# Channel-major products as 256-column matmuls onto one accumulator, and another first load

## The reference

```python
def reference(x, ...):
    hn = rmsnorm(h, norm_mix_w)
    z, xbc, dt_raw, u, g_a, g_b = split(hn @ w_in)        # 3072, 5120, 48, 1024, 2048, 2048 columns
    y_a = mamba2_mixer(z, xbc, dt_raw, ...)               # causal conv, silu, SSD over 8 groups, gated by silu(z)
    y_b = s5_mixer(u, ...)                                # complex scan per channel, gelu, GLU
    merged = sigmoid(g_a) * y_a + sigmoid(g_b) * y_b
    h = h + merged @ w_out
    h = h + conv_glu_ffn(rmsnorm(h), w_up, w_down)        # 5632 wide
    return rmsnorm(h)
```

## Time and profile before

| | |
|---|---|
| median of 3 runs | 1673.08 us |
| profiled execution | 1673.03 us |
| its span, first to last instruction | 1671.3 us |
| TensorE matmul busy | 1661.6 us, 99% of the span |
| VectorE busy | 1315.7 us, 79% |
| ScalarE busy | 984.2 us, 59% |
| granted TensorE clock, mean | 0.999 |

### The profile page before, as it was taken

How to read it: one execution, slowest core, us unless ns; L and a number is a source line. 1 busy time by engine, 2 the same in 40 slices (tenths; PEclk the granted TensorE clock), 3 DMA queues, 4 the chain that set the end, 5 groups by cost and what they waited for, 6 DMA issues and landing times.

```text
span 1671.3 us, 24189 instructions
## 1 busy us (share of the span) xinstructions
PE 1661.6 (99%) x8216; PEld 1386.3 (83%) x8216; DVE 1315.7 (79%) x1723; ACT 984.2 (59%) x1365; POOL 234.9 (14%) x337
## 2 busy tenths in 40 slices
PE   9999999999999999999999999999999999999998
PEld 8888888888888888888888888888888888888886
DVE  7999999999999996545766868888878888845544
ACT  7676676666677877444547754444444454454554
POOL 7843342221111110000000200000000000000001
PEclk9999999999999999999999999999999999999999
DMA  7666766666857666666787577777777777766564
GB/s 255 214 196 197 207 202 202 191 196 180 248 201 252 218 223 205 197 192 208 243 254 223 176 233 241 237 245 243 243 244 242 243 233 243 232 190 198 191 189 127
DMA packets 182873, 361.61 MB, mean 216 GB/s; under 512 B 17520, under 2 KB 45456, under 8 KB 182672
## 3 DMA queue, kind: packets, MB, share of 16 engines
q1 hardware_dynamic: 169264, 340.23, 64.0%
q0 software_dynamic: 12336, 19.92, 5.1%
q10 hardware_dynamic: 1200, 0.53, 0.1%
HBM read 335.41 MB, written 18.92 MB: 212 GB/s over the span
## 4 chain that ended last, share of the span: by engine, by line
PE 74%; DVE 2%; ACT 1%; issue 0%; DVEq 0%
PE psum L1930 23%; PE psum L1931 23%; PE psum L1932 23%; PE psum L1915 2%; PE psum L1917 1%; PE psum L2051 1%; DVE wlo L1216 1%; PE psum L2052 0%; DVE dec L1566 0%; ACT whi L740 0%; PE psum L2058 0%; PE psum L1966 0%; DVE dec L1562 0%; ACT xtok L949 0%; DVE zx L1629 0%
## 5 line engine op out<-in xcount | busy, mean ns | idle before, releaser
L740 ACT ACTIVATE whi<-raw 128x1024 fp32r<-128x1024 f32 x580 | 612.6, 1058 | 583.2 <-PE psum L1932 472.0
L1216 DVE TENSOR_TENSOR wlo<-raw,whi 128x1024 fp32r<-128x1024 f32 x580 | 708.8, 1228 | 312.6 <-ACT whi L740 305.9
L1915 PE MATMUL psum<-act,whi 128*128 128x512 f32 x1088 | 342.5, 396 | 0.0
L1930 PE MATMUL psum<-whi,nw 128*128 128x512 f32 x704 | 274.1, 389 | 0.0
L1931 PE MATMUL psum<-wlo,nw 128*128 128x512 f32 x704 | 273.9, 389 | 0.0
L1932 PE MATMUL psum<-whi,nw 128*128 128x512 f32 x704 | 273.9, 389 | 0.0
L1917 PEld LDWEIGHTS psum<-act,wlo 128*128 128x128 f32 x1088 | 204.4, 188 | 48.3
L1917 PE MATMUL psum<-act,wlo 128*128 128x256 f32 x1088 | 213.7, 278 | 0.0
L1915 PEld LDWEIGHTS psum<-act,whi 128*128 128x128 f32 x1088 | 165.6, 189 | 3.3 <-issue 3.2
L1932 PEld LDWEIGHTS psum<-whi,nw 128*128 128x128 f32 x704 | 132.1, 188 | 27.6
L1930 PEld LDWEIGHTS psum<-whi,nw 128*128 128x128 f32 x704 | 132.1, 188 | 27.3
(11 more groups left out here) (255 smaller groups left out, 2236.7 us busy)
## 6 DMA issues: line engine op xcount, KB each, us to landing
raw<-in_w_up SPq DMA_DIRECT2D x176, 512.0 KB, 4.8
raw<-in_w_zx SPq DMA_DIRECT2D x96, 512.0 KB, 3.7
raw<-in_w_down SPq DMA_DIRECT2D x88, 512.0 KB, 4.3
raw<-in_w_gate SPq DMA_DIRECT2D x64, 512.0 KB, 5.2
raw<-in_w_proj SPq DMA_DIRECT2D x48, 512.0 KB, 4.4
raw<-in_w_bc SPq DMA_DIRECT2D x32, 512.0 KB, 3.9
raw<-in_w_glu SPq DMA_DIRECT2D x32, 512.0 KB, 4.5
raw<-in_w_out SPq DMA_DIRECT2D x32, 512.0 KB, 4.7
```

What stands on the lines that cost most here:

```text
L740: fn(whi[:, s, :], raw[:, s, :], ACTF.Copy).then_inc(hi_ready, 1)
L1216: V.tensor_tensor(wlo[:, s, :], raw[:, s, :], whi[:, s, :], ALU.subtract).then_inc(lo_ready, 1)
L1915: mm(psum[:, b + t, :], whi[:, s, cols(t)], x, start=first, stop=False)
L1930: mm(banks[:, t, :], x_hi, high[:, k], start=first and k == 0, stop=False)
```

## The change

- `unit`: the 512-column product on `whi` becomes two of 256 columns (activation high, activation low) that go, like the product on `wlo`, to columns 0 to 255 of the bank. A quad is now six matmuls of 256 columns. The sum of a group stands finished in PSUM.
- ScalarE's `take_sums` replaces `take_hsum`: it copies the sum straight to `ub`, `bc` or `cpad`, or applies silu on the way to `zx` for z groups, and its `sum_ready` frees the banks. `add_halves`, `group_sums`, `u_sums`, `cpad_free` go from VectorE, the separate silu of z from ScalarE; `residual` adds the PSUM sum to `h` in one step, with no copy by ScalarE.
- SyncE first loads the first half of weight unit 0, then x's first piece, the second half, then unit 1, x's second piece and so on. ScalarE and VectorE make each half of `whi` and `wlo` ahead of the two activation rows. 13 small products stand at the start instead of 17.

```diff
@@ SyncE
+            sp.dma_start(raw[:, 0, 0:2 * L], a["w_u"][0][:, 0:2 * L]).then_inc(w_first, 16)
             for c in range(4):
                 sp.dma_start(xin[:, 4 * c:4 * c + 4, :], a["x"][:, 4 * c:4 * c + 4, :]).then_inc(x_in[c], 16)
-                sp.dma_start(raw[:, c, :], a["w_u"][c]).then_inc(w_in[c], 16)
+                if c == 0:
+                    sp.dma_start(raw[:, 0, 2 * L:], a["w_u"][0][:, 2 * L:]).then_inc(w_in[0], 16)
+                if c < 3:
+                    sp.dma_start(raw[:, c + 1, :], a["w_u"][c + 1]).then_inc(w_in[c + 1], 16)
@@ ScalarE
-            def take_hsum(g, end, gi=0, ui=0):
+            def take_sums(to, g, end, gi=0, ui=0, func=ACTF.Copy):
                 act.wait_ge(unit_used, ui + end)
-                if g:
-                    act.wait_ge(sum_ready, gi + g)
-                fn(hsum[:, :, :], sums(g, 1), ACTF.Copy).then_inc(hsum_ready, 1)
+                fn(to, sums(g), func).then_inc(sum_ready, 1)
...
+            def group_sums(name, i, r):
+                _, per, quads, u0, g0 = phase(name)
+                func = ACTF.Copy
+                if name == "u":
+                    to = ub[:, 2 * (r + 1):2 * (r + 1) + 2, :]
+                elif name == "zx" and r % 2 == 0:
+                    to, func = zx[:, ds(i * 4 + r, 2), 0, :], ACTF.Silu
+                elif comes_late(name, i, r):
+                    to = bc[:, i * 4 + r, :, :]
+                else:
+                    to = cpad[:, :, 3:3 + L]
+                take_sums(to, g0 + r, u0 + (r + 1) * quads, i * per, i * (per * quads), func)
@@ VectorE
-            def add_halves(to, g, gi=0):
-                dve.wait_ge(hsum_ready, gi + (g + 1))
-                V.tensor_tensor(to, sums(g, 0), hsum[:, :, :], ALU.add).then_inc(sum_ready, 1)
...
-                dve.wait_ge(hsum_ready, g + 1)
-                mul(hg, hg, hsum[:, :, :], ALU.add)
-                V.tensor_tensor(hg, sums(g, 0), hg, ALU.add).then_inc(sum_ready, 1)
+                dve.wait_ge(unit_used, UNIT0[name] + 4 * r + 4)
+                V.tensor_tensor(hg, sums(g), hg, ALU.add).then_inc(sum_ready, 1)
@@ TensorE
                     for t in tiles:
-                        mm(psum[:, b + t, :], whi[:, s, cols(t)], x, start=first, stop=False)
+                        mm(psum[:, b + t, 0:L], whi[:, s, cols(t)], x_hi, start=first, stop=False)
+                        mm(psum[:, b + t, 0:L], whi[:, s, cols(t)], x_lo, start=False, stop=False)
                     for t in tiles:
-                        ins = mm(psum[:, b + t, L:2 * L], wlo[:, s, cols(t)], x[:, 0:L], start=False, stop=last)
+                        ins = mm(psum[:, b + t, 0:L], wlo[:, s, cols(t)], x_hi, start=False, stop=last)
...
-            for k in range(17):
+            for k in range(13):
                 mm(WARM, ones[:, :], ones[:, :], start=True, stop=True)
```

More of the change, by code:

```diff
@@ L303, in group_bank, with sums @@
             return 2 * (g % 2)
-        def sums(g, half):
+        def sums(g):
             b = group_bank(g)
-            return psum[:, b:b + 2, half * L:half * L + L]
+            return psum[:, b:b + 2, 0:L]
         def chunk_banks(name, c):
@@ L768, in _ @@
             fn(rs[:, 0:1], ones[:, 0:1], ACTF.Copy)
[L769 removed]
             for c in range(4):
[L771 removed]
                 for half, done in ((0, half_hi), (1, hi_ready)):
+                    act.wait_ge(w_first if c == 0 and half == 0 else w_in[c], 16)
+                    w = slice(half * 2 * L, half * 2 * L + 2 * L)
+                    fn(whi[:, c, w], raw[:, c, w], ACTF.Copy).then_inc(done, 1)
+                    if c == 0 and half == 0:
+                        act.wait_ge(parm_in, 16)
+                    act.wait_ge(x_in[c], 16)
                     for k in range(4 * c + 2 * half, 4 * c + 2 * half + 2):
                         weighed_hi(k)
[L775 to L777 removed]
             for c in range(4):
@@ L781, in _ @@
                 split_hi(n)
-            take_hsum(0, 4)
-            def group_hsum(name, i, r):
+            take_sums(ub[:, 0:2, :], 0, 4)
+            def group_sums(name, i, r):
                 _, per, quads, u0, g0 = phase(name)
-                take_hsum(g0 + r, u0 + (r + 1) * quads, i * per, i * (per * quads))
+                func = ACTF.Copy
[8 more added lines that the diff above has]
+                take_sums(to, g0 + r, u0 + (r + 1) * quads, i * per, i * (per * quads), func)
             def normed_hi(c):
@@ L858, in group_silu @@
                 _, per, quads, u0, g0 = phase(name)
-                if name == "u":
+                if name == "u" or name == "zx" and r % 2 == 0:
                     return
[L861 to L865, removed]
+                if name == "zx":
                     act.wait_ge(conv_done, i * 2 + (r // 2 + 1))
@@ L896, in mixer_turn @@
                     last = name == "bc" and i == 1 and r == per - 1
-                    group_hsum(*before)
+                    group_sums(*before)
                     hi(0)
@@ L1248, in _ @@
                     V.tensor_tensor(wlo[:, c, w], raw[:, c, w], whi[:, c, w], ALU.subtract).then_inc(done, 1)
+                    if c == 0 and half == 0:
+                        dve.wait_ge(parm_in, 16)
+                    for k in range(4 * c + 2 * half, 4 * c + 2 * half + 2):
+                        weighed_lo(k)
             dve.wait_ge(wdt_in, 64)
@@ L1422, in s5_out @@
                 V.scalar_tensor_tensor(to, to, col("s5_d", blk), sums_at, ALU.mult, ALU.add).then_inc(y5_out, 1)
[L1424 to L1433, removed]
             def group_conv(name, i, r):
@@ L1467, in late_add @@
                     ins.then_inc(conv_done, 1)
[L1469 to L1474, removed]
             def x_turned(g):
@@ L1516, in mixer_turn @@
                         lo(2)
-                    cpad_free(*before)
                     s5_turn_on(r)
@@ L1520, in mixer_turn @@
                         last_state_sum(blk)
-                    if r == per - 1 and not last:
-                        group_sums(name, i, r)
                     if not last:
```

31 lines of the change are left out of this document (10 added, 21 removed).

## The result

The changed kernel takes **1686.38 us** (median of 6 runs, 1686.09 to 1686.87) against 1673.09 us before (6 runs on the same chip): ratio 1.008, 95% interval 1.0067 to 1.0093. It is 13.3 us slower, where the forecast was 7.3 us faster.

What follows compares the result with a forecast made beforehand. The prediction took TensorE's matmul pace to bound the kernel. Gains of 6.1 (quads), 0.8 (start) and 0.4 us (wait before L2010) summed to 7.3, taking 1673.1 to 1665.8 us, range 1660 to 1680.

Steps and rivals of the forecast that it cites:

- The bound: Whole kernel: between start and end it goes at the pace of TensorE's matmuls; VectorE follows closely without holding it.
- Term 1: 608 quads: six 256-column products at 0.1145 us each make a quad 0.687 instead of 0.697 us; gain 6.1 us.
- Rival 2: 608 quads: fixed cost per matmul makes a quad 0.733 us, 21.9 us lost, 1693.8 us; chance 0.15.
- its point of decision, 0.1165: Quads: the 256-column pitch in us from which a fixed cost per matmul decides against the change.
- the lower bound of half the wide pitch: Quads: 256 columns take half the 512-column pitch, 0.1132 us; quad 0.679 us, gain 10.9 us.
- The floor from the weight loads: Quads: weight loads limit the 256-column pitch, put at 0.108 to 0.118 us from sixteen 128-column products and their loads.
- Term 2: Start: half a weight unit ahead of x lets TensorE start at about 6.7 us, not 7.76; gain 0.8 us.
- Rival 4: Start: x's second piece comes late, TensorE waits between u0's units; 0.8 us less gain, 1666.6 us; chance within forecast's 0.60.
- The small products: Start, before u0: 13 instead of 17 end between 6.54 us and 1.3 us sooner, covered by the wait for x.
- Term 3: Group sums: ScalarE no busier, VectorE loses 38 steps, some 26 us, worth nothing itself; 0.4 us gained before L2010.
- Rival 1: Quads: loads or small per-matmul costs take the gain; pitch 0.1155 to 0.118 us, 1669.4 to 1678.6 us; chance 0.19.
- Rival 3: Gate phase after the mixer: VectorE and ScalarE lag, term 1's gain becomes waits before L2051; 1669 to 1672 us; chance 0.06.

Runs made afterwards that it cites:

- the split alone: Kernel before with only the 512-column product on `whi` split into two of 256, written to the two bank halves as before: 1686.19 us, ratio 1.0077.

## Why the prediction was wrong

**The bound: right.** The pace of the matmuls was named as what counts, and it is all that counted: 14.2 us from the quads against 13.3 measured, and 0.4 us of the difference is the wait at L2010.

**Term 1: wrong, and of the other sign.** The step that failed is "I take 0.1145 us, between the first two, nearer to the pair". The pair of 256-column products in the earlier trace rows is 0.23 us from its first start to the next wide product, but starts beside a change of length don't give the price, and only the quad's 0.697 was sure; in a long stream the pitch is 0.1200. That is 0.0055 us more on each of 3648 products than the prediction took, 20 us, and all but a little of the distance from 1665.8 to 1686.4. Rival 2 had the right reading, a cost beyond the columns for each matmul with its load, and its point of decision, 0.1165, was passed. Its size was too large: it charged the whole rest of the quad to the narrow products (0.1221, 21.9 us), while 0.6967 - 2 × (0.2267 + 0.1200) = 0.0034 us of the quad come with the mixture of lengths and don't follow into a uniform stream. So a quad gets two more constants, 0.0267 us, and is rid of 0.0034: 0.0233 us more. Columns / 2.4 GHz plus what the earlier trace rows leave, 0.2264 - 512 / 2400 = 0.0131, would have given 0.1198 us and 608 × (0.719 - 0.697) = 13.4 us. That sum was to be had from the rows; the lower bound of half the wide pitch assumed that nothing is fixed, which no row supported, and the range of 1660 to 1680 left rival 2 out.

The floor from the weight loads, 0.108 to 0.118 us, was too low: sixteen products of 128 columns are not a stream of 256-column ones. Both stand above the 107 ns for a load that the prediction took from the Trainium skill ("TensorE: Matmul & The Clock Gate", LDWEIGHTS), and on both sides only of half the wide pitch, 0.1132 us. The Trainium skill's N / 2.4 + 2.5 ns ("TensorE: Matmul & The Clock Gate", Back-to-back issue gap), which the page calls the gap of an isolated matmul, has the right shape and the right sign; the measured constant with a load of 128 columns beside each product is 13.3 ns, in three widths. It was weighed by its small number, and not for its shape.

**Term 2: the start came true, its gain didn't.** 6.7 us was forecast for the first product and 6.67 measured. The 0.8 us that should remain are 0 within what can be measured. Rival 4 was right: TensorE waits 0.7 us between units 0 and 1. The step "which takes ScalarE's lead but not much more" failed: x's second piece landed at 9.44 us, where before ScalarE could begin on it at 8.11, and unit 1 began at 10.52 instead of 10.70. The small products, costed at nothing, were so by a hair: the prediction let them end at 6.54 us or up to 1.3 sooner, and in this trace, at 1.2 GHz to their end, the last one starts at 6.56, 0.11 us before the first product of u0. That they didn't hold it up was luck.

**Term 3: sums by ScalarE.** That they cost TensorE nothing was right, and so was that what VectorE is rid of is worth nothing in itself. The 38 steps are as long as forecast (36 of 0.68 and 2 of 0.69 us, 26 us together); the busy time fell by 17 us only, since it counts instructions that overlap on record once. The 0.4 us before L2010 did go, but they went in the split alone too, so ScalarE's copies can't be given them.

**Rival 1** is decided against: the pitch was beyond its range (0.118), with loads of 64 columns it fell to 0.1133 and not to the 0.107 to 0.110 of a product freed from its load, and the same 0.0133 us stand at 384 and 512 columns, where products are further apart than loads follow each other in the earlier trace rows. **Rival 3** couldn't show itself, since TensorE came to the gate phase later and not sooner.

No version here that does all of the work is faster than the kernel before. An estimate of the room in the channel-major units, from these pitches, is 608 × (0.697 - 3 × 0.2267) = 10 us, for a form with three products of 512 columns a quad, as the token-major units have it; that was not tried.

## What to carry to other kernels

Where TensorE sets the pace and each product brings a weight load, count matmuls as well as columns: splitting a 512-column product costs a fixed sum (here 0.0133 us with loads of 128 columns), times all of them, less the little that a mixture of lengths had cost before (here 0.0034 us in a quad), and work taken off engines that don't bound the kernel pays nothing of it back. Take the cost of one instruction from a long uniform stream, or from the sum over a whole period, never from neighbouring starts in a mixed one. And a first product that starts earlier is a gain only if what the second and third need lands earlier too.

## What the runs showed of the hardware

- Pitch in a uniform stream of fp32r products, a load of 128 columns each, full clock: 256 columns 0.1200 us, 384 columns 0.1733, 512 columns 0.2267.
- The constant depends on the load and not in one direction: at 256 columns, loads of 128, 96, 64 and 32 columns give 0.120, 0.116, 0.113 and 0.116 us; at 384 columns 0.1733 with 128 and with 64; at 512 columns a load of 64 gives 0.230 instead of 0.227. Why is open.
- A mixture of 512 and 256 columns takes 0.697 us a quad, against 0.693 from the uniform pitches, and 0.707 with the lengths in turn; in the mixed quad a load of half the length saves nothing (0.700 us a quad, 1674.05 us with 64).
- Products on the same 256 columns of a bank, 0.12 us apart, cost no more than where the high and the low activation go to different halves of it (1686.38 against 1686.19 us, 0.1200 us from start to start in both).
